# One transformer layer's projections, block compression and output steps laid between the pieces of its 32 attention heads

## The reference, cut to what matters

```python
def nsa_attention(h, w_in, w_out, cmp_pos, cmp_w1, cmp_w2, rel_table):
    q, kc, vc, ks, vs, kw, vw, gate = jnp.split(h @ w_in, splits, axis=-1)   # 16 heads, 4 kv groups, width 64
    kc_b = compress_kv(to_kv(kc), cmp_pos[0], cmp_w1[0], cmp_w2[0])          # 15 blocks of 32 tokens, 2-layer MLP
    vc_b = compress_kv(to_kv(vc), cmp_pos[1], cmp_w1[1], cmp_w2[1])
    s_cmp = jnp.einsum("bsgrd,bngd->bgrsn", q, kc_b).astype(jnp.float32) * scale
    p_cmp = masked_softmax(s_cmp, cmp_end[None, :] <= t[:, None])
    o_cmp = jnp.einsum("bgrsn,bngd->bsgrd", p_cmp.astype(vc_b.dtype), vc_b)
    ...                                     # 4 blocks of 64 tokens and top-k 16: every causal block is selected
    o_slc = selected_block_attention(q, to_kv(ks), to_kv(vs), sel_idx, rel_table)
    o_win = banded_attention(q.reshape(B, S, N_HEADS, dh), to_kv(kw), to_kv(vw), rel_table, B_WINDOW)
    g = jax.nn.sigmoid(gate.astype(jnp.float32)).reshape(B, S, N_HEADS, 3)
    o = g[..., 0:1] * o_cmp + g[..., 1:2] * o_slc + g[..., 2:3] * o_win
    return o.reshape(B, S, -1) @ w_out
```

## Time and profile before

| | us |
|---|---|
| median of 3 runs | 3479.1 |
| lowest and highest of them | 3475.09, 3480.41 |
| the profiled execution | 3480.2 |
| its span, first to last instruction | 3478.1 |
| PE busy in the span | 3352.5 |
| DVE busy | 2099.3 |
| ACT busy | 1716.9 |
| mean granted clock of PE | 0.983 |

### The profile page before, as it was taken

How to read it: one execution, slowest core, us unless ns; L and a number is a source line. 1 busy time by engine, 2 the same in 40 slices (tenths; PEclk the granted TensorE clock), 3 DMA queues, 4 the chain that set the end, 5 groups by cost and what they waited for, 6 DMA issues and landing times. The chain is left out here.

```text
span 3478.1 us, 53492 instructions
## 1 busy us (share of the span) xinstructions
PE 3352.5 (96%) x20376; PEld 2963.9 (85%) x20376; DVE 2099.3 (60%) x2315; ACT 1716.9 (49%) x2279; POOL 81.0 (2%) x180
## 2 busy tenths in 40 slices
PE   8999999999999999999999999899999999999899
PEld 6899988888998888887888888788888888888787
DVE  5567565656766555566565564665656755656655
ACT  4456444444664444455444433454445544445544
POOL 0000000000000000000000000000000000000000
PEclk9999999999999999999999987999999999999999
DMA  6665445555554555553555542245555445555354
GB/s 243 219 222 206 147 174 187 187 191 184 196 179 149 190 192 183 181 185 143 182 193 182 181 158 79 81 182 191 183 191 194 147 170 192 182 192 189 128 192 170
DMA packets 105214, 618.78 MB, mean 178 GB/s; under 512 B 10832, under 2 KB 19152, under 8 KB 34800
## 3 DMA queue, kind: packets, MB, share of 16 engines
q1 hardware_dynamic: 84288, 562.07, 44.8%
q10 hardware_dynamic: 20784, 54.71, 4.7%
HBM read 615.62 MB, written 9.50 MB: 180 GB/s over the span
## 5 line engine op out<-in xcount | busy, mean ns | idle before, releaser
L1291 DVE TENSOR_TENSOR wlo<-raw,whi 128x2048 fp32r<-128x2048 f32 x526 | 1204.7, 2291 | 657.8 <-ACT whi L760 655.5
L1982 PE MATMUL ps<-xhl,whi 128*128 128x512 f32 x3456 | 1201.9, 396 | 0.0
L760 ACT CAST whi<-raw 128x2048 fp32r<-128x2048 f32 x526 | 1001.1, 1904 | 204.7 <-PE ps L2118 108.7
L1986 PE MATMUL ps<-xhl,wlo 128*128 128x256 f32 x3456 | 893.1, 279 | 0.0
L1982 PEld LDWEIGHTS ps<-xhl,whi 128*128 128x128 f32 x3456 | 626.5, 188 | 121.7
L1986 PEld LDWEIGHTS ps<-xhl,wlo 128*128 128x128 f32 x3456 | 651.6, 189 | 37.5
L2117 PE MATMUL ps<-wlo,ht 128*128 128x512 f32 x1056 | 417.1, 395 | 0.0
L2116 PE MATMUL ps<-whi,ht 128*128 128x512 f32 x1056 | 417.1, 395 | 0.0
L2118 PE MATMUL ps<-whi,ht 128*128 128x512 f32 x1056 | 416.6, 394 | 0.0
L2097 PE MATMUL ps<-xhl,whi 128*128 128x256 f32 x1360 | 393.7, 289 | 9.4 <-DVE qb L1701 5.4
L2099 PE MATMUL ps<-xhl,wlo 128*128 128x256 f32 x1360 | 388.3, 286 | 0.0
(11 more groups left out here) (299 smaller groups left out, 3868.0 us busy)
## 6 DMA issues: line engine op xcount, KB each, us to landing
raw<-stream SPq DMA_DIRECT2D x528, 1024.0 KB, 4.8
bias<-rel_bias ACTq DMA_DIRECT2D x80, 256.0 KB, 2.6
gain<-gains ACTq DMA_DIRECT2D x19, 1024.0 KB, 4.8
bias<-fixed_bias ACTq DMA_DIRECT2D x40, 256.0 KB, 3.2
rel_bias<-rel_vectors SPq DMA_DIRECT2D x16, 512.0 KB
x<-x_tokens ACTq DMA_DIRECT2D x1, 1024.0 KB, 5.0
y_tokens<-x ACTq DMA_DIRECT2D x1, 1024.0 KB, 3.9
s<-constants ACTq DMA_DIRECT2D x1, 512.0 KB, 6.5
```

What stands on the lines that cost most here:

```text
L760: nc.scalar.copy(whi[:, slot, :], raw[:, slot, :]).then_inc(sem["hi_ready"], 1)
L1291: nc.vector.tensor_tensor(wlo[:, slot, :], raw[:, slot, :], whi[:, slot, :].bitcast(F32), ALU.subtract).then_inc(sem["lo_ready"], 1)
L1982: wide = lambda: pe.matmul(ps[:, bank, 0:2 * half], hi[:, k, col0:col0 + P], src[:, k0 + k, :], start=first and k == 0, stop=last and k == ...
L1986: e = pe.matmul(ps[:, bank, 0:half], lo[:, k, col0:col0 + P], src[:, k0 + k, 0:half], start=False, stop=False)
```

## The change

The nine phases become one, `nsa`, in 35 turns. Its items are listed by hand with the PSUM bank that each writes and the engine that empties it, and `NSA_SLOTS` says how many pieces lie in each turn. The 32 heads go in groups: four selected heads and then four window heads of the same kv group. There are no `keep_busy` calls inside. PE reads q from `q2` directly; POOL clears `vblk` and `pcmp` instead of DVE; ACT copies the compression's sources (L1504 and L1505 before, on DVE) and the compressed keys and values; the gates are a tanh with a DVE pass for the rest of the sigmoid; the output of the compressed attention is added to `o` in turn 22 rather than being its first content. Before the next phase `arrive` issues 18 filler transposes instead of 5.

```diff
+def nsa_items():
+    one = lambda kind, at, bank, by: Item(kind, at, 1, (bank,), 4, by)
+    items = [one("v", 0, 4, "act"), one("q", 0, 5, "dve"), one("k", 0, 6, "dve"), Item("gate", 0, 1, (7,), 2, "act"),
+             one("cmp", 0, 4, "act"), one("cmp", 1, 5, "act"), one("k", 4, 6, "dve"), one("v", 256, 7, "act"),
+             one("q", 4, 4, "dve"), Item("hidden", 0, 2, (5, 6), 4, "dve"), one("q", 8, 7, "dve"),
+             Item("hidden", 1, 2, (4, 5), 4, "dve"), one("q", 12, 6, "dve"), Item("blocks", 0, 0, (4,), 1, "act"),
+             Item("cmp_scores", 0, 0, (7,), 1, "dve"), Item("cmp_turn", 0, 0, (5, 6), 1, "act"), Item("cmp_values", 0, 0, (7, 4), 1, "add"),
+             Item("cmp_values", 1, 0, (5, 6), 1, "add")]
+    items += [Item("out", i, 1, (), 4, "") for i in range(4)]
...
+NSA_EARLY = 4
+NSA_HEADS = 2 * HEADS
+NSA_SLOTS = slots_of([(n, part) for n in range(NSA_EARLY, len(NSA) - 1) for part in range(NSA[n].parts)][:-1],
+                     [4, 4, 4, 2, 2, 2, 2, 2, 2, 2, 2, 2, 2, 2, 3, 0, 1, 0, 0, 1, 1, 1, 0, 0, 0, 2, 2, 2, 2, 0, 1, 1, 1, 0, 0])
+NSA_TURNS = {23: 0, 24: 1, 25: 2, 26: 3, 27: 4, 29: 5, 32: 6, 34: 7}
+NSA_GELU = 13
+NSA_ADD = 22
...
         elif i % 3 == 1:
-            project(t("v", 0, 256, 8, 1, 1), f("q", 0, 4), f("cmp", 0, 2))
-            add("compress", ("pe", "act", "dve"), 4,
...
-            project(f("k", 0, 1), f("k", 4, 1), t("v", 256, 256, 8, 1, 1), t("gate", 0, 48, 8, 1, 1))
-            add("cmp_attend", ("pe", "act", "dve"),
...
-            attend("nsa_slc", HEADS, "causal", 0)
-            attend("nsa_win", HEADS, "causal", 0)
+            nsa()
...
-        if i % 3 == 1:
-            turn(0, 8)
-            wout()
```

ACT's turn, with `empty(n)` behind the last piece of an item:

```diff
+                for t in range(ph.n + 3):
+                    here = NSA_SLOTS[t]
+                    first = (len(here) + 1) // 2
+                    if t in NSA_TURNS:
+                        turned(NSA_TURNS[t], (t + 1) % 2)
+                    if t == NSA_GELU:
+                        gelu()
+                    follow(here[:first])
+                    if t < ph.n:
+                        exps(t)
+                    if 1 <= t <= ph.n:
+                        turned_probs(t - 1)
+                    follow(here[first:])
```

DVE: the blocks follow the items `k` 4 and `v` 256, the compressed softmax the item `cmp_scores`:

```diff
+                def empty(n):
+                    item = NSA[n]
+                    if item.kind in ("q", "k"):
+                        low_heads(n)
+                    if item.kind == "gate":
...
+                    elif (item.kind, item.at) == ("k", 4):
+                        blocks_made(0)
+                    elif (item.kind, item.at) == ("v", 256):
+                        blocks_made(1)
+                    elif item.kind == "hidden":
...
+                    elif item.kind == "cmp_scores":
+                        compressed_probs(n)
...
+                def compressed_added():
+                    for qt in range(TT):
+                        dve.wait_ge(sem["cmp_pv"], B["cmp_pv"] + qt + 1)
+                        dve.wait_ge(sem["o_done"], B["o_done"] + NSA_ADD - 2)
+                        for g in range(KVG):
+                            made = ps[:, NSA[place(NSA, "cmp_values", qt)].banks[g // 2], g % 2 * T:g % 2 * T + T]
+                            to = o[:, qt, g * T:g * T + T]
+                            if 8 * g + 4 < NSA_ADD:
+                                e = nc.vector.tensor_tensor(to, made, to, ALU.add)
+                            else:
+                                e = nc.vector.tensor_copy(to, made)
+                            e.then_inc(sem["cmp_added"], 1)
...
+                for t in range(ph.n + 3):
+                    here = NSA_SLOTS[t]
+                    first = (len(here) + 1) // 2
+                    if t < ph.n:
+                        biased(t)
+                    if t == NSA_ADD:
+                        compressed_added()
+                    if t in NSA_TURNS:
+                        turned(NSA_TURNS[t], (t + 1) % 2)
+                    follow(here[:first])
+                    if 1 <= t <= ph.n:
+                        inverted(t - 1)
+                    follow(here[first:])
+                    if 2 <= t <= ph.n + 1:
+                        heads_out(t - 2)
```

PE: the waits of a head's pieces, and the order of a turn:

```diff
+                def scores(t):
+                    group, kind, h_ = nsa_head(t)
+                    kept(place(NSA, "q", 4 * group))
+                    kept(place(NSA, "k", 4 * kind))
+                    if t >= 2:
+                        pe.wait_ge(sem["biased"], B["biased"] + t - 1)
+                    k = NSA_TURNS.get(t - 1)
+                    if k is not None:
+                        pe.wait_ge(sem["lo_made"], B["lo_made"] + k + 1)
...
+                def values(t):
+                    group, kind, h_ = nsa_head(t)
+                    pe.wait_ge(sem["pt_ready"], B["pt_ready"] + t + 1)
+                    wait(pe, sem["o_done"], B["o_done"] + t)
...
+                def turn_heads(k, t):
+                    pe.wait_ge(sem["cmp_added"], B["cmp_added"] + 8)
+                    pe.wait_ge(sem["o_done"], B["o_done"] + nsa_tile_done(k))
...
+                for n in range(1, NSA_EARLY):
+                    for part in range(NSA[n].parts):
+                        part_of(n, part)
+                for t in range(ph.n + 3):
+                    here = NSA_SLOTS[t]
+                    first = (len(here) + 1) // 2
+                    if t < ph.n:
+                        scores(t)
+                    if t in NSA_TURNS:
+                        turn_heads(NSA_TURNS[t], t)
+                    for n, part in here[:first]:
+                        part_of(n, part)
+                    if 1 <= t <= ph.n:
+                        turn_probs(t - 1)
+                    for n, part in here[first:]:
+                        part_of(n, part)
+                    if 2 <= t <= ph.n + 1:
+                        values(t - 2)
+                for i, quarter in ((3, 0), (3, 1), (2, 3), (3, 2), (3, 3)):
+                    out(i, quarter)
...
-                    keep_busy(18 if before_of(last).kind == "weave" else 5 if last.after == "post" or last.final else 0, 3)
+                    keep_busy(18 if before_of(last).kind in ("weave", "nsa") else 5 if last.after == "post" or last.final else 0, 3)
```

More of the change, by code:

```diff
@@ L1082, in high_heads @@
                         nc.scalar.copy(v[:, :, 512:512 + P], ps[:, bank, T:2 * T].rearrange("p (t c) -> p t c", t=TT))
-                    for rows, other, q, k, heads, nt in heads_of(item):
+                    for rows, other, q, k, heads, nt in heads_of(item, ph):
                         made = ps[rows, bank, 0:nt * T].rearrange("p (i t) -> p i t", i=nt)
@@ new lines, in nsa @@
+                for n in range(NSA_EARLY):
+                    ahead(ph, NSA[n].step)
+                    empty(n)
+                for t in range(ph.n + 3):
[13 more added lines that the diff above has]
+                        heads_out(t - 2)
@@ L1964, in _ @@
+            run(dve, "dve", dict(setup=setup, between=between, ffn=ffn, mix=mix, nsa=nsa, weave=weave))
         @block.tensor
```

933 lines of the change are left out of this document (449 added, 484 removed).

## The result

The changed kernel takes 3415.96 us in the median of four runs (3411.28 to 3419.24), the kernel before, on the same chip, 3478.39. The ratio is 0.982, with a 95% interval of 0.980 to 0.984: 62.4 us less, where 58 were forecast. The profiled execution is one of 3416.29 us with a span of 3414.5, against 3478.1 before.

What follows compares the result with a forecast made beforehand. PE bounds the kernel, busy 96%, but the changed layer's 264.6 us held only 161 of full-clock work. 161 plus 44.1 of stalls gave 205; with 1.4 for later fillers, net 58.2 less: 3421 us, range 3408 to 3434 at 0.50.

Steps and rivals of the forecast that it cites:

- content: Changed layer: the work PE must issue at full clock, summed over projections, gate, compression, scores, output and heads: 161 us.
- 1 gate: Gate step in fourth place: its 48 products and some of the first compression product lose time to a fallen clock, 3.2 us.
- Item 2: Turns 2 and 3: DVE's ordered work outlasts PE's, so PE stands about 5.6 us, then a clock fall of 1.7: 7.3.
- Item 3: Turns 4 to 14, nearly level between PE and DVE: 15% on 54 us, taken from the next layer's turns: 8 us.
- Item 4: Turns 15 to 18: scores wait for ACT copies (1.4), half clock (4.8), softmax chain wait (5.4), together 13.6; bounds 8 and 20.
- 5 turns 19 to 24: Light turns: adding the compressed output on DVE 3.4, empty turns paced by one head's chain 3.1, together 6.5 us.
- Item 6: Phase end: last heads have too few quarters beside them, and the last pair's chain precedes the last output step: 5.5 us.
- 14.2 over 27.5: Four hidden compression steps, 128 products: 27.5 us if still at 1.2 GHz, 14.2 at 0.11 us each; 14.2 was taken.
- Rival B: Clock stays at 1.2 GHz in hidden steps and through turns 13 to 24, adding 13.3 and 10 us: 3444; chance 0.16.
- Rival A: PE sets the pace everywhere, items 3 and 5 cost 1 together, item 2 is covered: kernel 3400 us; chance 0.16.
- rival C: Heads and products alternate but the head's chain is uncovered, 2.75 us a turn; gain from seams and clock alone: 3436; chance 0.14.
- D: Without fillers PE's clock stays at 1.2 GHz all phase, slower than before: 342 us, or 3559; chance 0.03 with slower mixtures.

Runs made afterwards that it cites:

- run without overlap: Changed kernel with all projection and compression quarters ahead of turn 1 and all output quarters behind the last head, none beside the heads: 3448.93 us, ratio 0.9914.
- versions with the copies cut: Changed kernel with DVE's block copies cut into halves: at the ends of turns 3 to 6, 3418.71 us; in DVE's gaps, 3416.09 us; also combined with other edits.
- copies in the gaps: Changed kernel with halves of the block copies put where DVE waits for ACT, in turns 1, 2, 6 and 9: 3416.09 us, ratio 0.9825.
- first and second tries: Changed kernel with, first, DVE's division ahead of k parts and block copies in turns 2 and 4: 3418.65 us; second, block copies cut, ending turns 3 to 6: 3418.71.

## Why the prediction was right, step by step

The time (3421 against 3416) and the mechanism hold. Each item beside what the trace of after shows; content is what PE must issue at full clock, from the prediction's prices:

| item | charged | measured |
|---|---|---|
| 1 gate | 3.2 | 3.0 (2005.26 to 2038.05 is 32.8 for 29.8; in two variants it was 1.5) |
| 2 turns 2 and 3 | 7.3 | 7.2 (wait 5.36, the rest clock) |
| 3 turns 4 to 14 | 8 | 1.6 |
| 4 turns 15 to 18 | 13.6 | 13.3 (26.75 for 13.5) |
| 5 turns 19 to 24 | 6.5 | 6.9 (21.71 for 14.8) |
| 6 the end | 5.5 | 8.2 (45.12 for 37.0) |

**The content.** 161 us in the prediction, and 161 laid out by turns. The products stand 0.12 us apart and the hidden ones 0.11 where the clock is at 1.00, as forecast. The choice of 14.2 over 27.5 for the hidden steps was right for most, and the reason I gave (they are bound by their weight load) was not what it hung on: it hung on the clock. With a wait of 0.7 us or more among them the clock fell to 1.2 GHz in every version that had one; without a wait it fell in turn 8 of the changed kernel and among the second 64 of the run without overlap, and did not in turns 11 and 12 of the changed kernel. What decides between these last I can't say from the runs. Rival B was nearer than its chance of 0.16 says; the versions with the copies cut fell into it for 17 and for 10 us (2087.9 to 2098.1 with the copies in the gaps).

**Item 2.** The order on DVE was read rightly, 5.36 for 5.6. The first and second tries show what the sum did not say: this wait cannot simply be taken away, since DVE's turns 2 to 4 are full and the next head stands behind.

**Item 3** was mis-sized: 8 charged, 1.6 measured. The 57.1 us of turns 4 to 14 have 54.2 of content; 1.3 of the rest is the clock behind the wait of turn 3 and belongs to item 2. What is left is smaller than the clock fall at 2079.6 to 2086.4, worth 3.4 in turns 8 and 9 (6.37 and 6.42 against 5.02 and 4.35), because some other turns took less than the prices (5.92 for 6.7 in turn 14). The step that failed is taking the 15% of the earlier trace rows over (78 of 90.3 is 14% less, which is 16% on top). In the trace of before those 12 us are mostly single events, waits of PE that sum to 8.9 us (one of 3.9, two of about 2) and a granted clock of 0.94 over the stretch, and not a share of every turn; waits of that size did not occur here. The turns themselves are 4.35 and 5.02 us at full clock, without a gap on PE. Rival A, that PE sets the pace, is true in turns 5 to 13.

**Item 4.** The scores took 12.06 us for 64, and the wait behind them 3.51 in two pieces. 13.6 was right as a sum, by luck. Inside it I had 2 us for the scores' clock where 5.0 were lost (12.06 less 7.1), 5.4 for the wait where 3.5 were, and 1.4 for ACT's copies where the one wait in turn 15 is 0.25: errors that cancel.

**Item 6** was too low by 2.7. I had counted the last chain of values, division, transposes and splitting, which shows as waits of 0.98, 1.22, 0.67, 0.67 and 1.01 us between 2187 and 2196.5 (4.6 together), and one of 0.83 ahead of turn 30. I had not counted that the output products behind it run at half rate, until 2202.5 (the granted clock is 0.51 from 2195.6 to 2202.5), some 3 us. It is the same as in item 2, where I charged it: a stretch with waits is followed by one at half rate.

So 161 + 44.1 = 205 was 6.4 too high in item 3, 2.7 too low in item 6 and 0.3 too high in the rest: 201.1. The 1.4 for the fillers ahead of the next phase was right (2.16 in place of 0.74).

**Where the 62 us come from.** By the run without overlap, 29.1 us of the phase (272.6 less 243.5) come without any overlap, from the seams, the hidden steps' clock and the fillers between the stages, and 33.2 from the pieces beside the heads. With fillers in that run's head turns the parts are 38.8 and 23.5, but 5.5 us of this difference lie ahead of the first filler, so the shares are known to some 10 us only. The prediction did not part them; rival C put the second part at 15. That the fillers' going alone brings nothing was measured; which of the seams brings how much of the first part was not, nor what POOL's copies of q, the copies that ACT took over or the moved addition bring. One seam shows in the trace of before: PE waited 3.27 us for the first copy of q (L724), up to 2148.01.

**Rivals.** A falls outside turns 5 to 13, and the clock fall takes 3.4 us from it within them. B falls for the changed kernel in its light turns (0.74 in turns 19 to 24, where B had 0.50) and for all but the last few of its hidden products. C falls by 33 us. D is far: the phase's granted clock is 0.85, the same as before, and the stretches at 0.50 are together some 61 of its 201 us.

## What to carry to other kernels

When heads and products are interleaved, count each engine's instructions turn by turn in queue order, not only the bottleneck's: the one large wait stood where DVE's order took 11 us (2043.2 to 2054.3, 1.4 of it waiting for ACT) against PE's 7, and moving one instruction moved the wait. Price a short wait by what runs behind it: a wait of 1.49 us in turn 3, ahead of wide products, cost 1.6 in that turn and, in three of the four versions that had it, 1.4 more in the next, where the clock fell; 0.71 us, and 1.11 with 0.61, among narrow ones cost 5 to 8 beyond themselves, since the clock then stayed down longer. Filling with real work gives both the covered chain and the clock; fillers give only the clock and take PE time themselves, and before the two came out even.

## What the runs showed of the hardware that I had not expected

- Filler transposes alone took the granted clock from 0.50 to 1.00 in bare head turns (19 us each in the two kernels without overlap), and their removal took it from 0.91 to 0.64 in the head turns of the kernel before. The time followed in both: 2.7 us less with fillers in turns 4 to 10 of the first pair, 6.6 us more without them in the second, where the fillers' own time ahead of the heads was 5.3.
- Narrow products in one row brought the clock down with PE busy throughout: from 1.00 to 0.50 after 4.1 and 6.5 us of products of 120 and 60 columns (2084.5 in the run without overlap, 2082.8 with fillers in it). In the changed kernel, with heads' pieces between, it fell once, at 2079.6, and was back at 2086.4, behind 256-column products. With the copies cut it was back only 17 us after the fall (2070.0 to 2087.0); a wait of 1.11 us stood ahead of that fall, one of 0.61 us and 32 more such products behind it.
- With the same instructions ahead of it, the phase began between 2003.0 and 2010.0 us in the fourteen profiles, and inside it the last stretch, from turn 31 on, varied from 20.0 to 23.0 us. Several single edits worth 3 to 5 us in the phase are not resolved by medians of four for that reason.
